# First mixers: one quarter of a depthwise convolution on TensorE, as products of 128 rows by 32 columns instead of products with diagonal matrices

## The reference, cut to what matters

```python
u = rms_norm(h, norm_mix[i])
q, k, v, c, g = jnp.split(u @ w_in[i], splits, axis=-1)
...
c_val, c_gate = jnp.split(c, 2, axis=-1)
c = c_val * jax.nn.sigmoid(c_gate)
c = depthwise_conv(c, conv_w[i], conv_b[i])      # y[t, ch] = sum over tap of c[t + tap - 15, ch] * w[tap, ch], plus b[ch]
c = jax.nn.silu(layer_norm(c, conv_ln_g[i], conv_ln_b[i]))
y_conv = c @ w_conv_out[i]
```

## Time and profile before

| | |
|---|---|
| runs (3) | 1759.19, 1759.76, 1760.83 us; median 1759.76 |
| the profiled execution | 1759.31 us |
| its span, first to last instruction | 1757.5 us |
| TensorE busy | 1744.6 us (99%), 9886 MATMUL records |
| VectorE, ScalarE, GpSimd busy | 1157.1, 930.6, 26.5 us |
| mean granted TensorE clock | 0.999 of 2.4 GHz |
| DMA | 303 MB, 172 GB/s on average |

### The profile page before, as it was taken

How to read it: one execution, slowest core, us unless ns; L and a number is a source line. 1 busy time by engine, 2 the same in 40 slices (tenths; PEclk the granted TensorE clock), 3 DMA queues, 4 the chain that set the end, 5 groups by cost and what they waited for, 6 DMA issues and landing times.

```text
span 1757.5 us, 26168 instructions
## 1 busy us (share of the span) xinstructions
PE 1744.6 (99%) x9886; PEld 1528.9 (87%) x9886; DVE 1157.1 (66%) x1700; ACT 930.6 (53%) x1376; POOL 26.5 (2%) x32
## 2 busy tenths in 40 slices
PE   9999999999999999999999999999999999999998
PEld 8888898898888988889889888889898888989886
DVE  6665588766655766568776665578575656857473
ACT  6554456655544555455655554467563546755352
POOL 0000000000000000000000000000000000000000
PEclk9999999999999999999999999999999999999999
DMA  8754523444545544552355445444265543435551
GB/s 314 219 192 169 214 102 139 175 176 183 192 170 190 210 183 173 190 198 101 128 190 189 183 173 192 163 157 163 99 213 192 192 165 112 152 120 194 202 181 48
DMA packets 45842, 303.04 MB, mean 172 GB/s; under 512 B 5104, under 2 KB 6256, under 8 KB 12312
## 3 DMA queue, kind: packets, MB, share of 16 engines
q1 hardware_dynamic: 45720, 301.36, 48.3%
HBM read 300.02 MB, written 1.31 MB: 171 GB/s over the span
## 4 chain that ended last, share of the span: by engine, by line
PE 97%; DVE 1%; ACT 1%; issue 1%; POOLq 0%; POOL 0%; ACTq 0%; DVEq 0%
PE psG L498 13%; PE psG L500 13%; PE psG L499 13%; PE psG L576 9%; PE psP L576 5%; PE psSO L576 5%; PE psG L582 5%; PE psG L549 3%; PE psG L550 3%; PE psG L551 3%; PE psSO L582 3%; PE psP L582 3%; PE psSO L693 2%; PE psP L615 1%; PE psSO L906 1%; PE psSO L500 1%
## 5 line engine op out<-in xcount | busy, mean ns | idle before, releaser
L1608 DVE TENSOR_TENSOR wlo<-raw,whi 128x1024 fp32r<-128x1024 f32 (+4 forms) x388 | 656.3, 1704 | 312.0 <-ACT whi L1086 311.8
L1086 ACT ACTIVATE whi<-raw 128x1024 fp32r<-128x1024 f32 (+4 forms) x388 | 554.1, 1444 | 276.3 <-PE psG L500 162.1
L498 PE MATMUL psG<-whi,x 128*128 128x512 f32 (+3 forms) x544 | 210.6, 387 | 0.0
L500 PE MATMUL psG<-whi,x 128*128 128x512 f32 (+3 forms) x544 | 200.9, 369 | 0.0
L499 PE MATMUL psG<-wlo,x 128*128 128x512 f32 (+3 forms) x544 | 200.5, 369 | 0.0
L498 PE MATMUL psG<-whi,hid_hi 128*128 128x512 f32 x472 | 184.1, 390 | 0.0
L500 PE MATMUL psG<-whi,hid_lo 128*128 128x512 f32 x472 | 183.6, 389 | 0.0
L499 PE MATMUL psG<-wlo,hid_hi 128*128 128x512 f32 x472 | 183.6, 389 | 0.0
L576 PE MATMUL psG<-x,whi 128*128 128x512 f32 x704 | 179.8, 392 | 0.0
L549 PE MATMUL psG<-x,wlo 128*128 128x256 f32 x512 | 147.5, 288 | 1.4 <-DVE wlo L1608 1.4
L576 PEld LDWEIGHTS psG<-x,whi 128*128 128x128 f32 x704 | 126.6, 189 | 22.6
(11 more groups left out here) (382 smaller groups left out, 2773.0 us busy)
## 6 DMA issues: line engine op xcount, KB each, us to landing
raw<-in_w SPq DMA_DIRECT2D x261, 1024.0 KB, 4.8
raw<-in_w SPq DMA_DIRECT2D x12, 768.0 KB, 4.2
raw<-in_w SPq DMA_DIRECT2D x14, 512.0 KB, 3.3
raw<-in_w SPq DMA_DIRECT2D x4, 576.0 KB, 3.8
raw<-in_w SPq DMA_DIRECT2D x4, 432.0 KB, 3.2
bias<-line_scratch SPq DMA_DIRECT2D x8, 192.0 KB, 10.3
h<-in_x SPq DMA_DIRECT2D x2, 512.0 KB, 5.9
out<-h SPq DMA_DIRECT2D x2, 512.0 KB, 2.7
```

The lines of the kernel that those rows point to most:

```text
L498: e.matmul(o, ph, wh, start=first, stop=False)
L500: i = e.matmul(o, pl, wh, start=False, stop=last)
L1086: e.activation(w_at(whi, j, off, n), raw[:, j % RAW, off:off + n], ACT.Copy).then_inc(s_hi, count)
L1608: e.tensor_tensor(w_at(wlo, j, off, n), raw[:, j % RAW, off:off + n], f32(w_at(whi, j, off, n)), ALU.subtract).then_inc(s_lo, count)
```

## The change

The 31 taps of chunk 1 are grouped in eight groups of four successive taps (the last of three), and the 128 channels in four groups of 32. One product has 128 rows, which are four taps of 32 channels each, and 32 columns, which are the 32 channels; the stationary matrix is four small diagonals below each other. The four channel groups write to partitions 0 to 31, 32 to 63, 64 to 95 and 96 to 127 of `O`, so they stand in different columns of the array. That makes 8 times 4 = 32 products a layer of 128x32 by 256 positions, for 31 of 128x128 by 256.

- The moving operand `fours` (in `thg[:, 1]`) holds, for each channel group g, four copies of its 32 rows of `pad`, the copy j shifted by j positions. SP makes it with 16 DMAs a layer, from SBUF to SBUF, 32 rows of 284 floats each. They stand in SP's queue behind one more weight load, and wait for `pad`.
- The stationary matrices `quad` (in `thg[:, 0, 0]`) are made by VectorE with two instructions a layer ahead of c0[1]: a `tensor_reduce` of `ident` to 128x32 and a multiplication of 128x1024.
- ScalarE's 31 diagonal matrices a layer go. Its copy of the sum comes two ticks later.
- TensorE's generator yields four times, then has four bursts of eight products (two groups of taps), at the fifth to eighth tick.
- The taps' weights lie in the constants in another layout.

```diff
@@ tensor @@
             def conv_taps(l):
-                yield
+
+                for _ in range(4):
+                    yield
                 for s, v in free["SO"][1]:
                     e.wait_ge(s, v)
-                e.wait_ge(s_pad, 2 * l + 1)
-                for tap in range(TAPS):
-                    n = TAPS * l + tap + 1
-                    e.wait_ge(s_dgc, n)
-                    e.matmul(O[:, 0:256], diag[:, tap % 16, :], pad[:, 1, tap:tap + 256], start=tap == 0, stop=tap == TAPS - 1).then_inc(s_cv, 1)
-                    if tap % 5 == 4:
+                e.wait_ge(s_quad, l + 1)
+                e.wait_ge(s_fours, 256 * (l + 1))
+                for m in range(8):
+                    n = 128 if m < 7 else 96
+                    for g in range(4):
+                        i = e.matmul(O[32 * g:32 * g + 32, 0:256], quad[0:n, 4 * m + g, :], fours[0:n, g, 4 * m:4 * m + 256], start=m == 0, stop=m == 7)
+                        if m == 7:
+                            i.then_inc(s_cv, 1)
+                    if m % 2 == 1:
                         yield
                 free["SO"][1] = [(s_acc3, l + 1)]
@@ scalar @@
             def conv_taps(l):
-                for tap in range(TAPS):
-                    n = TAPS * l + tap + 1
-                    if tap >= 16:
-                        e.wait_ge(s_cv, n - 16)
-                    e.activation(diag[:, tap % 16, :], ident, ACT.Copy, scale=k("conv_w", (l * 4 + 1) * 31 + tap)).then_inc(s_dgc, 1)
-                    if tap % 5 == 4:
-                        yield
-                yield
-                e.wait_ge(s_cv, TAPS * l + TAPS)
+                for _ in range(9):
+                    yield
+                e.wait_ge(s_cv, 4 * l + 4)
                 e.activation(acc[:, 1, :], O[:, 0:256], ACT.Identity, bias=k("conv_b", 4 * l + 1)).then_inc(s_acc3, 1)
@@ vector, mixer1, between q[0] and c0[1] @@
+                v = step(e.tensor_reduce(eyes, ident.rearrange("p (j n) -> p n j", j=4), AX.X, ALU.add))
                 e.memset(pad[:, :, 0:15], 0.0).then_inc(s_pad0, 1)
...
+                e.wait_ge(s_dv, v)
+                e.tensor_tensor(quad, eyes.rearrange("p (o n) -> p o n", o=1).to_broadcast([128, 32, 32]),
+                                k("conv_t", 32 * l, 32).rearrange("p (i o) -> p i o", o=1).to_broadcast([128, 32, 32]), ALU.mult).then_inc(s_quad, 1)
                 use(c0[1])
@@ sync @@
             for l in range(LAYERS):
+                load(NUM[halves("w_in", l, (768, 1024), (1280, 1536))[1]] + AHEAD + RAW + 1)
+
+                e.wait_ge(s_pad0, 2 * l + 2)
+                e.wait_ge(s_pad, 2 * l + 1)
+                for g in range(4):
+                    for j in range(4):
+                        n = 284 if j < 3 else 283
+                        e.dma_start(fours[32 * j:32 * j + 32, g, 0:n], pad[32 * g:32 * g + 32, 1, j:j + n]).then_inc(s_fours, 16)
                 load(NUM[halves("w_o", l, cols(1))[1]] + AHEAD + RAW)
```

More of the change, by code:

```diff
@@ L243, in columns @@
         ("norm_ffn1", 16), ("norm_mix", 16), ("norm_ffn2", 16), ("norm_pe", 16), ("ln1_g_2", 16), ("ln2_g_2", 16),
-        ("q_norm", 2), ("k_norm", 2), ("sink", 16), ("conv_w", 248), ("conv_b", 8), ("conv_ln_g", 8),
+        ("q_norm", 2), ("k_norm", 2), ("sink", 16), ("conv_w", 186), ("conv_t", 64), ("conv_b", 8), ("conv_ln_g", 8),
         ("conv_ln_b", 8), ("mla_q_norm_g_2", 6), ("mla_kv_norm_g_2", 2), ("diff_subln_g_2", 2), ("diff_lambda_2", 256),
@@ L337, in build @@
         s_lw = sem("s_lw")
-        s_pad0, s_cg, s_cth, s_cvl, s_pad, s_dgc, s_cv, s_acc3, s_acc = (
-            sem(n) for n in ("s_pad0", "s_cg", "s_cth", "s_cvl", "s_pad", "s_dgc", "s_cv", "s_acc3", "s_acc"))
+        s_pad0, s_cg, s_cth, s_cvl, s_pad, s_quad, s_fours, s_cv, s_acc3, s_acc = (
+            sem(n) for n in ("s_pad0", "s_cg", "s_cth", "s_cvl", "s_pad", "s_quad", "s_fours", "s_cv", "s_acc3", "s_acc"))
         s_lnc, s_nmu, s_lnq, s_lnv, s_lnr, s_ln, s_z, s_ychi, s_yclo = (
@@ L397, in build @@
         thg, qs, qn, kv, qT, kT, acc = (M1[n] for n in ("thg", "qs", "qn", "kv", "qT", "kT", "acc"))
-        diag = flat(thg[:, 1, :, :]).rearrange("p (i n) -> p i n", i=16)
+        fours = flat(thg[:, 1, :, :])[:, 0:4 * 284].rearrange("p (g n) -> p g n", g=4)
+        eyes = flat(thg[:, 1, :, :])[:, 1152:1184]
+        quad = thg[:, 0, 0, :].rearrange("p (i n) -> p i n", n=32)
         qa, ka, va, rt, cq, kr, vc, kb, vb, qbT, kbT, mix = (
@@ L1778, in tap_of @@
                 def tap_of(ch, tap, a, own, bias):
-                    x, w = pad[:, ch, tap:tap + 256], k("conv_w", (l * 4 + ch) * 31 + tap)
+                    x, w = pad[:, ch, tap:tap + 256], k("conv_w", (l * 3 + (0, None, 1, 2)[ch]) * 31 + tap)
                     if own is None:
@@ L2510 @@
     put("diff_lambda_2", np.broadcast_to(a["diff_lambda_2"].reshape(1, 256), (128, 256)))
-    put("conv_w", a["conv_w"].reshape(2, 31, 4, 128).transpose(3, 0, 2, 1).reshape(128, 248))
+    taps = a["conv_w"].reshape(2, 31, 4, 128)
+    put("conv_w", taps[:, :, (0, 2, 3)].transpose(3, 0, 2, 1).reshape(128, 186))
+    quads = np.zeros((2, 32, 128), np.float32)
+    quads[:, :31] = taps[:, :, 1]
+    put("conv_t", quads.reshape(2, 8, 4, 4, 32).transpose(2, 4, 0, 1, 3).reshape(128, 64))
     onehot, mask, c2 = tables()
```

## The result

| | before | changed |
|---|---|---|
| median of 8 runs | 1759.45 us (1759.02 to 1760.83) | 1754.48 us (1753.48 to 1755.22) |
| the profiled execution, its span | 1759.31, 1757.5 us | 1753.7, 1751.9 us |
| mean granted TensorE clock | 0.999 | 0.997 |

The ratio is 0.9972, with a 95% interval from 0.9962 to 0.9981: faster by 5.0 us or 0.28%, where 12.5 us were forecast. The time lies in the stated range, but 7.5 us of the forecast gain are missing.

The account below looks back on a forecast made before the run. TensorE was taken to bound the kernel, with 97% of the last chain of waits. Per layer, 8.3 us saved on products less 1.8 of waiting gave -6.5, two layers -13: 1746.4 profiled, 1747 us median; range 1742 to 1756.

Parts of the forecast that it names:

- What a product costs: TensorE's taps: four products in different columns cost 0.431 us, as one does; with detours a layer saves 8.3 us.
- A detour: TensorE, going over to the new products and back: 0 to 0.41 us on each of four a layer, 0.41 taken.
- Half as wide: Rival, TensorE's taps: only neighbouring products' passes overlap, 0.216 us a product, a layer saves 3.1 us: 1753 us; chance 12%.
- In turn: Rival, TensorE's taps: columns take turns, a burst is 3.86 us, 3.8 us a layer slower: 1767 us; chance 14%.
- I take 0.47: SP's 16 copies issued 0.47 us apart, last at 228.7, landed at 230.8; TensorE waits 1.8 us a layer.
- The bound on the other side: Upper bound on TensorE's wait for the copies: 4.7 us, with 0.63 to 0.66 an issue or 4.9 a landing.
- its three signs of being wrong: On TensorE: first wait over 5 us, a detour much above 0.41, or new idle time between 250 and 314.
- The copies' cover: SP's 19 loads behind the copies wait until about 229.2 at no cost; cover gone beyond some 10 us more.
- What is late next: VectorE, 220.4 to 250.0, just full; turns have 5.0 us of cover, could wait 1.5 us a layer; 0 taken.
- the late copies: Rival, SP: slow issue and landing make TensorE wait 7 us a layer: 1757; 8%, shared with other lost gains.

Follow-up runs that it names:

- the run by groups: One-burst kernel with products reordered: all eight of one channel group, then the next group's, instead of four neighbours in different columns; 1755.56 us, ratio 0.9979.
- The filled wait: Changed kernel with 34 products of 128x128 by 256, adding nothing to the result, ahead of TensorE's wait for the copies; 1752.07 us, ratio 0.9958.
- the later bursts: Changed kernel with TensorE's four bursts two ticks later (seventh to tenth) and ScalarE's copy of the sum at its twelfth tick; 1743.52 us, ratio 0.9909.
- the copies first: Changed kernel with the 16 copies moved ahead of the weight load they stood behind in SP's queue; 1743.73 us, ratio 0.9911.
- one burst: Changed kernel with all 32 products of a layer together at the eighth tick, ScalarE's copy at its eleventh; 1743.70 us, ratio 0.9911.
- one burst and one tick of pause: One-burst kernel with VectorE's taps paused for one tick in c1[1] (4 taps, 1.6 us); 1740.89 us, ratio 0.9895.

## Why the prediction was right and wrong

**What a product costs: right.** Four products in different columns cost what one does. Records stand in fours 0.007 us apart, as the text said they would (some 0.01). A detour costs 0.33 us, not the 0.41 of the pairs on different rows. The Trainium skill's 3.07 for four products on different rows (TensorE: Matmul & The Clock Gate, Part 3, the table of measured speedups) would have made a round an estimated 0.56 us. Here, for four in different columns, it is 0.43, so this case measures the full factor of 4.

**Half as wide: refuted.** In each round all four first passes start ahead of all second passes: four records start within 0.02 us, and the run by groups shows that the records of one group follow each other by some 0.216. The number alone would not have told: 1754.48 is nearer to this rival's 1753 than to the forecast. The rule of the same page of the Trainium skill (Part 3, what overlaps and what doesn't) that matmuls start in program order does not hold for the two passes of a float32 product here, and the run by groups shows a start out of order across three records.

**In turn: refuted**, and with it the idea that weight loads of column groups cannot overlap: line 699's loads are 109 ns long, and four of them go by in each 0.216 us, beside running products. The rule that would have the loads stand open was that of the same page of the Trainium skill (Part 3, what overlaps and what doesn't), and the measurement decides against it.

**The step that failed: "I take 0.47", the distance of the copies' issues.** Measured 0.63, with one of 1.28 in the first layer. That moved the last landing from 230.8 to 233.7 and the wait from 1.8 us to 4.7 and 3.9. The landing of the last copy (2.1 forecast, 1.9 measured) and the start (221.7) were right. The bound on the other side had 0.63 to 0.66 for the eight DMAs of `bias`, and 4.7 us of wait. That it came true is luck. The 0.63 was 5.07 / 8, an average over DMAs of unlike length (ns min/median/max):

```profile
L2424 SPq DMA_DIRECT2D bias<-line_scratch x8: 423/444/1506, 54.6 to 59.2; - x8
```

Of their seven distances five are 0.47 to 0.49, the others 0.69 and 1.55. So the trace before had no row with a steady 0.63. Its other DMA of 32 rows (`rb`, 5.81 to 6.38) had 0.57, and the text left it out. The form of the copies, 32 rows from SBUF to SBUF, stood in no row, and 0.47 had no more behind it than 0.57. What makes an issue of this form cost 0.63 no run shows: all runs have the same 16 copies, and fewer or wider ones were not tried.

The two waits together took 5.0 us more than forecast (8.6 for 3.6).

**The step that was missing: what idle time does to the clock.** The text priced the wait at its length and put the clock at nothing. A wait of 4.7 or 3.9 us costs 1.7 us more, because TensorE goes on at 1.2 GHz for a while afterwards (3.4 us in either layer, by the granted clock). That took another 3.4 us. It is why 1754.48 lies above the 1743 to 1753 that the text gave for products side by side with a wait of up to 4.7 us, and none of its three signs of being wrong came up: the first wait was under 5 us, the detour under 0.41, and TensorE had no new idle time between 250 and 314. The two steps make 5.0 + 3.4 = 8.4 us; the cheaper detour gave back 0.6 (17.2 for 16.6); 7.5 are missing. The filled wait shows it: same wait, same start of the burst, clock at full speed, and the first layer has its 1.7 us back. The kernel before could not show it, since TensorE there never idles this long inside the program: its longest wait is 1.4 us, and the clock stays at full speed behind it.

**The copies' cover: right.** A load that is 7.2 us late costs TensorE nothing.

**What is late next: right in the stretch, wrong in the waiter.** I had VectorE "just full" in that stretch and looked for the damage at the turns. In the changed kernel it does not show, since TensorE's wait lets VectorE catch up: it is busy 5.00 of the 5 us from 229 to 234. As soon as that wait is gone, the first to miss VectorE is the turn of k: 0.6 us in one layer with the later bursts, 0.3 and 0.7 with the copies first, 1.6 in each with one burst. Only the version with one burst and one tick of pause has it all: 1759.20 - 1740.89 = 18.3 us. The sum for it is 17.2 for the products in four bursts and 6 x 0.33 = 2.0 for the detours it does without, 19.2. Of the last 0.9 us about half lies at the start: in the profiled execution of this kernel the first product of the weights (line 552) starts at 10.22 us, that of before (line 549) at 9.76. The rest stays open.

**Small slips of the text.** The chances of the cases faster than before add up to at most 0.66 + 0.12 = 0.78, where it has 0.79. The 16.5 us that the late copies eat from are 2 x 8.3 = 16.6. Neither changes the forecast.

## What to carry to other kernels

Where a bound engine gets a new input that another queue has to bring, the issue of each small DMA counts before its bytes do: count the issues, and put them in front of loads that nobody is waiting for. Their distance is best measured on DMAs of the same form; an average over a few others hides both the usual distance and the slow ones, and where no row has the form, the term is a range. A wait on TensorE can cost more than its length (here 1.7 us more behind waits of 3.9 and 4.7), so work that runs ahead of its input is better moved by a tick or two. But what TensorE gains has to be followed to the engine that is nearly full: moving 1.6 us of VectorE's work by one tick gave 2.8 us, moving 3.2 us of it by two ticks cost 2.1. And independent small products belong next to each other in the program, one for each group of columns: in another order the same products took three times as long.

## What the runs showed of the hardware that I had not expected

Copies of 32 rows of 1136 bytes from SBUF to SBUF take 0.59 us each on SP's queue and follow each other by 0.63, where the weight loads of 1 MB next to them take 0.33. One of the sixteen in the first layer takes longer, 1.24 us in the changed kernel and 0.93 to 1.59 in the other nine traces; in the second layer one does so in two of the ten (1.55 and 0.77). Float32 products on all rows and 32 columns run four at once at no loss, 0.432 us a round, with 0.33 us for going over and back. Records of a product can start while three earlier ones in the program have not. Waits of TensorE of 3.9 and 4.7 us were followed by 3.4 us at half clock; of the waits of 1.9 to 2.0 us some were (in three runs) and some were not, and those of 1.4 and 1.6 us never.
